# Output projections from seven block products, with their weight blocks split by three engines

## The reference, cut to what matters

```python
merged = sigmoid(a_r) * y_r + sigmoid(a_f) * y_f      # tokens x 1024, y = heads @ w_o
x = x + merged @ w_out[l]                             # 1024 x 1024 times 1024 x 1024
h2 = rmsnorm(x, g_ffn[l])                             # block 1: feeds the FFN
# block 2 ends with: return rmsnorm_2(x + merged @ w_out_2, final_norm_g_2)
```

## Time and profile before

| | us |
|---|---|
| median of 3 runs | 3062.49 |
| the profiled execution, its own time | 3061.24 |
| its span, first to last instruction | 3059.5 |
| TensorE busy | 2936.4 (96%) |
| VectorE, ScalarE, GpSimd busy | 1511.6, 1038.7, 946.5 |
| mean granted TensorE clock | 0.985 |

### The profile page before, as it was taken

How to read it: one execution, slowest core, us unless ns; L and a number is a source line. 1 busy time by engine, 2 the same in 40 slices (tenths; PEclk the granted TensorE clock), 3 DMA queues, 4 the chain that set the end, 5 groups by cost and what they waited for, 6 DMA issues and landing times.

```text
span 3059.5 us, 38358 instructions
## 1 busy us (share of the span) xinstructions
PE 2936.4 (96%) x14282; PEld 2348.0 (77%) x14282; DVE 1511.6 (49%) x2003; ACT 1038.7 (34%) x1732; POOL 946.5 (31%) x725
## 2 busy tenths in 40 slices
PE   7989999999999999999998999999999999999998
PEld 6778777788787788887887766668788888788886
...
GB/s 128 42 43 59 18 28 18 93 45 48 60 95 136 92 83 81 78 90 195 48 46 129 97 8 21 15 40 104 83 76 80 82 71 80 73 158 48 45 110 86
DMA packets 107877, 224.13 MB, mean 73 GB/s; under 512 B 14048, under 2 KB 27104, under 8 KB 106848
## 3 DMA queue, kind: packets, MB, share of 16 engines
q1 hardware_dynamic: 67680, 134.01, 14.5%
...
...
## 4 chain that ended last, share of the span: by engine, by line
PE 78%; DVE 12%; ACT 5%; issue 2%; POOL 2%; DMA 1%; ACTq 0%; POOLq 0%; SPq 0%; DVEq 0%
PE ps L356 17%; PE ps L372 13%; PE ps L2050 12%; PE ps L317 12%; PE ps L2172 8%; PE ps L1085 3%; PE ps L1116 1%; PE ps L2376 1%; DVE mla_ptl L1049 1%; ACT ps L1025 1%; PE ps L1101 1%; DVE mla_nm L1058 1%; PE ps L1103 1%; PE ps L1102 1%; POOL wl L3379 1%
## 5 line engine op out<-in xcount | busy, mean ns | idle before, releaser
L3377 POOL TENSOR_TENSOR wh<-raw,zeros 128x512 fp32r<-128x512 f32 x356 | 400.5, 1125 | 2077.7 <-PE ps L372 559.2
L3379 POOL TENSOR_TENSOR wl<-raw,wh 128x512 fp32r<-128x512 f32 x356 | 532.8, 1497 | 27.9
L372 PE MATMUL ps<-hth,wh 128*128 128x512 f32 x704 | 285.3, 405 | 2.1 <-DVE fox_vl L1298 2.1
L372 PE MATMUL ps<-hth,wl 128*128 128x512 f32 x704 | 279.2, 397 | 0.0
L372 PE MATMUL ps<-htl,wh 128*128 128x512 f32 x704 | 278.8, 396 | 0.0
L317 PE MATMUL ps<-wh,hth 128*128 128x512 f32 (+2 forms) x608 | 237.3, 390 | 12.4 <-POOL wl L3379 7.7
L317 PE MATMUL ps<-wl,hth 128*128 128x512 f32 (+2 forms) x608 | 234.1, 385 | 0.0
L317 PE MATMUL ps<-wh,htl 128*128 128x512 f32 (+2 forms) x608 | 233.8, 385 | 0.0
L356 PE MATMUL ps<-hth,wh 128*128 128x512 f32 x496 | 196.6, 396 | 0.4 <-issue 0.3
L356 PE MATMUL ps<-hth,wl 128*128 128x512 f32 x496 | 196.3, 396 | 0.0
L356 PE MATMUL ps<-htl,wh 128*128 128x512 f32 x496 | 196.2, 395 | 0.0
...
## 6 DMA issues: line engine op xcount, KB each, us to landing
raw<-in_stream_dram SPq DMA_DIRECT2D x356, 256.0 KB, 2.6
up_raw<-in_stream_dram SPq DMA_DIRECT2D x21, 1024.0 KB, 5.8
...
norm_x<-in_x_dram ACTq DMA_DIRECT2D x1, 4096.0 KB, 15.8
...
```

The source lines that it names most:

```text
L372: ins = nc.tensor.matmul(ps[:, bank + half, :], w[:, j, c:c + P], a[:, k, HALF * half:HALF * half + HALF], start=k == 0 and q == 0, stop=k ...
L3377: nc.gpsimd.tensor_tensor(wh[:, s, :], raw[:, s, :], zeros[:].to_broadcast([P, HALF]), ALU.add).then_inc(w_hi, 1)
L3379: nc.gpsimd.tensor_tensor(wl[:, s, :], raw[:, s, :], wh[:, s, :], ALU.subtract).then_inc(w_split, 1)
```

## The change

The projection is written as seven block products instead of eight. The merged activations have four blocks: P (features 0 to 511, tokens 0 to 511), Q (features 512 to 1023, the same tokens), R and S (the same for tokens 512 to 1023). The weight has e, f (rows 0 to 511, column half 0 and 1) and g, h (rows 512 to 1023). VectorE forms, in M and in new tiles, s1 = R+S, s2 = s1-Q, s3 = Q-S, s4 = P-s2, and w1 = h-g, w2 = f-w1, w3 = f-h, w4 = e-w2. The seven products are P e, Q g, s1 w1, s2 w2, s4 f, s3 w3, R w4, each of 4 feature groups x 4 token tiles x 3 = 48 matmuls, 336 in all; sums are formed in PSUM and in X.

Only e and f come through the stream and GpSimd (8 units for a projection, `U_OUT` 16 -> 8). The other five weight blocks (g, w1, w2, w3, w4) are split by ScalarE (`Wh`) and VectorE (`Wl`). TensorE's order of units of 12 matmuls is `SEQUENCE`; e alternates with g, and f with w2 and w3. f is loaded once beside the stream, for w2 and w3. h and g are loaded at the start of the merge stage (`early_loads`, g into slot 1 of `sg`) and subtracted there (`early_sum`, w1); ScalarE's second pair of sigmoids waits for that. g is loaded once more for its own split, h once more for w3, e for w4. The residual comes in two DMAs of 2 MB. The norm goes by halves of the tokens: tiles 4 to 7 take their second-half columns first. `Down` keeps its own order of transposes. Below, the diff cut to its core; `tt` is a tensor_tensor on VectorE (subtract unless it says add), `low(w, x, j)` waits for ScalarE's `h{w}.j` and makes `l{w}.j`, and removed bodies are those named above.

```diff
+def out_units(a):
+    for ks, c in ((K1, 0), (K1, 1)):
+        for k in ks:
+            unit(rows(a, k, HALF * c, HALF))
+out_units(w["w_out"][0])
...
+OUT_BLOCKS = N_UNITS + 4 * (PAIRED + 1)
+N_ALL = OUT_BLOCKS + 2 * 16
+K1, K2 = range(0, 4), range(4, 8)
...
+    self.Wh = sb(name + "_wh", [P, 4, HALF], F32R, scope)
+    self.Wl = sb(name + "_wl", [P, 4, HALF], F32R, scope)
+    self.Ml = sb(name + "_ml", [P, KT, S], F32R, scope)
+    self.S1h = sb(name + "_s1h", [P, 4, HALF], F32R, scope)
+    self.S2h = sb(name + "_s2h", [P, 4, HALF], F32R, scope)
...
+def late_square(self, act, summed, t, last):
+    summed(act, t, last)
+    n = len(self.squares)
+    if n >= 2:
+        self.a.wait(act, self.squares[-2])
+    self.squares.append(f"sq{last}.{t}")
+    self.a.did(nc.scalar.activation(self.junk[:, n % 2, :], self.X[:, t, self.later(t) if last else self.early(t)], ACT.Square,
+                                    accum_out=self.ss[:, last, t:t + 1]), f"sq{last}.{t}")
+def late_root(self, act, summed, t):
+    self.late_square(act, summed, t, 1)
+    self.a.wait(act, f"sq1.{t}")
+    self.v.wait(act, f"base{t // 4}")
+    self.a.did(nc.scalar.activation(self.r[:, 0, t:t + 1], self.ss[:, 1, t:t + 1], ACT.Sqrt, scale=1.0 / D, bias=self.base[:, t:t + 1]), f"rt{t}")
+def late_warm(self, act):
+    self.a.wait(act, "sq0.3")
+    self.a.did(nc.scalar.activation(self.r[:, 0, 0:1], self.ss[:, 0, 0:1], ACT.Sqrt), "warm")
+def late_base(self, dve, n):
+    ts = slice(4 * n, 4 * n + 4)
+    self.a.wait(dve, f"sq0.{4 * n + 3}")
+    self.v.did(nc.vector.tensor_scalar(self.base[:, ts], self.ss[:, 0, ts], 1.0 / D, EPS, ALU.mult, ALU.add), f"base{n}")
+def late_gains(self, dve, ts):
+    if ts[0] == 0:
+        dve.wait_ge(self.gain_in, 16)
+    for t in ts:
+        at = self.X[:, t, self.early(t)]
+        self.v.did(nc.vector.tensor_tensor(at, at, self.G[:, self.early(t)], ALU.mult), f"xg{t}")
...
-    self.pa.wait(act, "a1", KT - 1)
-    for k in range(KT):
-        self.v.wait(act, "sum", k)
-        nc.scalar.activation(hth[:, k, :], self.M[:, k, :], ACT.Copy).then_inc(self.ch, 1)
...
+SEQUENCE = ("e0 g0 e1 g1 e2 g2 e3 g3 w1.0 w1.1 w1.2 w1.3 w2.0 w2.1 f0 w2.2 f1 w2.3 f2 w3.0 f3 w3.1 w3.2 w3.3").split()
+PRODUCT = dict(e="pe", g="qg", w1="s1w1", w2="s2w2", f="s4f", w3="s3w3")
...
+    self.P, self.Q, self.R, self.S = M[:, 0:4, t1], M[:, 4:8, t1], M[:, 0:4, t2], M[:, 4:8, t2]
+    self.f = norm.XN[:].rearrange("p a (b n) -> p (a b) n", b=2)
+    self.low = lambda k: norm.Ml[:, 4 * (k // 2):4 * (k // 2) + 4, (t1, t2)[k % 2]]
...
+def early_loads(self, act):
+    act.dma_start(self.norm.F[:], self.weights(K2, 1)).then_inc(self.early_in, 16)
+    for br in range(2):
+        act.dma_start(self.merge.sg[:, br, 1, :].rearrange("p (a n) -> p a n", a=2), self.weights(K2[2 * br:2 * br + 2], 0)).then_inc(self.early_in, 16)
+def early_sum(self, dve):
+    dve.wait_ge(self.early_in, 48)
+    for br in range(2):
+        at = self.norm.F[:, 2 * br:2 * br + 2, :]
+        self.v.did(nc.vector.tensor_tensor(at, at, self.merge.sg[:, br, 1, :].rearrange("p (a n) -> p a n", a=2), ALU.subtract), "w1" + "ab"[br])
+def g(self, br):
+    return self.merge.sg[:, br, 0, :].rearrange("p (a n) -> p a n", a=2)
+def early_summed(self, act):
+    self.v.wait(act, "w1b")
+    a, v, p, m, n = self.a, self.v, self.p, self.merge, self.norm
+    def copy(out, x, step):
+        a.did(nc.scalar.activation(out, x, ACT.Copy), step)
+    def high(w, x, j, product):
+        if product:
+            p.wait(act, f"{product}.u{j}" if j < 3 else f"{product}.3")
+        copy(n.Wh[:, j, :], x[:, j, :], f"h{w}.{j}")
+    last = KT - 1
+    m.pa.wait(act, "a1", last)
+    for k in range(last):
+        m.v.wait(act, "sum", k)
+        to = slice(0, S if k < 4 else HALF)
+        copy(hth[:, k, to], m.M[:, k, to], f"hi{k}")
+    for br in range(2):
+        act.dma_start(self.g(br), self.weights(K2[2 * br:2 * br + 2], 0)).then_inc(self.g_in, 16)
+    m.py.wait(act, "y0", last)
+    act.dma_start(n.X[:, 0:4, :], self.source[:, 0:4, :]).then_inc(self.x_in[0], 16)
+    act.wait_ge(self.g_in, 32)
+    m.py.wait(act, "y1", last)
+    act.dma_start(self.f, self.weights(K1, 1)).then_inc(self.f_in, 16)
+    for j in range(4):
+        copy(n.Wh[:, j, :], self.g(j // 2)[:, j % 2, :], f"hg.{j}")
+    m.v.wait(act, "sum", last)
+    copy(hth[:, last, 0:HALF], m.M[:, last, 0:HALF], f"hi{last}")
+    v.wait(act, "s1b")
+    copy(n.S1h[:], self.R, "s1h")
+    high("w1", n.F, 0, "qg")
+    v.wait(act, "s3b")
+    copy(hth[:, 4:8, HALF:S], self.S, "s3h")
+    n.load(act)
+    act.dma_start(n.X[:, 4:8, :], self.source[:, 4:8, :]).then_inc(self.x_in[1], 16)
+    high("w1", n.F, 1, "qg")
+    v.wait(act, "lg.3")
+    copy(n.S2h[:], self.Q, "s2h")
+    high("w1", n.F, 2, "qg")
+    high("w1", n.F, 3, "qg")
+    v.wait(act, "w2")
+    high("w2", n.F, 0, "s1w1")
+    for t in range(4):
+        n.late_square(act, self.summed, t, 0)
+    high("w2", n.F, 1, "s1w1")
+    high("w2", n.F, 2, "s1w1")
+    p.wait(act, "s1w1.3")
+    act.dma_start(self.R, self.weights(K2, 1)).then_inc(self.h_in, 16)
+    copy(n.S1h[:], self.P, "s4h")
+    v.wait(act, "s3l")
+    act.dma_start(self.S, self.weights(K1, 0)).then_inc(self.e_in, 16)
+    high("w2", n.F, 3, "s1w1")
+    n.late_warm(act)
+    v.wait(act, "w3")
+    for j in range(4):
+        high("w3", self.R, j, "s2w2")
+    for t in range(4):
+        n.late_root(act, self.summed, t)
+    for j, t in ((0, None), (1, 0), (2, None), (3, 1), (None, 2), (None, 3)):
+        if j is not None:
+            high("w4", self.S, j, "s3w3")
+        if t is not None and not n.final:
+            n.high(act, t)
+            self.store(act, t)
+    for t in range(4, NT):
+        n.late_square(act, self.summed, t, 0)
+    if n.final:
+        for t in range(4, NT):
+            n.late_root(act, self.summed, t)
+        return
+    for t in range(4, NT):
+        n.late_root(act, self.summed, t)
+        if t > 4:
+            n.high(act, t - 1)
+            self.store(act, t - 1)
+    n.high(act, last)
+    self.store(act, last)
...
+    def add(k, t):
+        bank, tile, c = dict(pe=(0, 0, 0), qg=(4, 0, 0), s1w1=(0, 4, 1), s2w2=(4, 0, 1), s4f=(0, 0, 1), s3w3=(4, 4, 1), rw4=(4, 4, 0))[k]
+        p.wait(dve, f"{k}.{t}")
+        at = n.X[:, tile + t, HALF * c:HALF * c + HALF]
+        tt(at, at, ps[:, bank + t, :], f"{k}.{t}", ALU.add)
+    for k in range(4):
+        a.wait(dve, f"hi{k}")
+        tt(htl[:, k, :], M[:, k, :], hth[:, k, :], f"lo{k}")
+    m.column(dve, KT - 2, 0, M[:, KT - 2, :])
+    m.v.wait(dve, "sum", KT - 2)
+    v.wait(dve, "lo3")
+    tt(M[:, 0:3, t2], M[:, 0:3, t2], M[:, 4:7, t2], "s1a", ALU.add)
+    v.wait(dve, "s1a")
+    tt(M[:, 4:7, t2], M[:, 4:7, t1], M[:, 4:7, t2], "s3a")
+    m.gated(dve, last, 1, M[:, last, :], 0)
+    a.wait(dve, "hi6")
+    tt(htl[:, 4:7, t1], M[:, 4:7, t1], hth[:, 4:7, t1], "loqa")
+    m.gated(dve, last, 1, M[:, last, :], 1)
+    low_g(0)
+    m.total(dve, last, M[:, last, :])
+    low_g(1)
+    m.v.wait(dve, "sum", last)
+    tt(M[:, 3, t2], M[:, 3, t2], M[:, 7, t2], "s1b", ALU.add)
+    a.wait(dve, "hi7")
+    tt(htl[:, 7, t1], M[:, 7, t1], hth[:, 7, t1], "loqb")
+    v.wait(dve, "s1b")
+    tt(M[:, 7, t2], M[:, 7, t1], M[:, 7, t2], "s3b")
+    v.wait(dve, "s3b")
+    tt(self.Q, self.R, self.Q, "s2")
+    low_g(2)
+    a.wait(dve, "s1h")
+    v.wait(dve, "s2")
+    tt(self.low(1), self.R, n.S1h[:], "s1l")
+    low_g(3)
+    low("w1", n.F, 0)
+    low("w1", n.F, 1)
+    tt(self.P, self.P, self.Q, "s4")
+    a.wait(dve, "s2h")
+    v.wait(dve, "s4")
+    tt(self.low(2), self.Q, n.S2h[:], "s2l")
+    low("w1", n.F, 2)
+    dve.wait_ge(self.x_in[0], 16)
+    for t in range(4):
+        add("pe", t)
+    low("w1", n.F, 3)
+    dve.wait_ge(self.f_in, 16)
+    v.wait(dve, "lw1.3")
+    tt(n.F[:], self.f, n.F[:], "w2")
+    for t in range(4):
+        v.wait(dve, f"pe.{t}")
+        add("qg", t)
+    v.wait(dve, "w2")
+    for j in range(3):
+        low("w2", n.F, j)
+    a.wait(dve, "s3h")
+    tt(htl[:, 4:8, t2], self.S, hth[:, 4:8, t2], "s3l")
+    dve.wait_ge(self.x_in[1], 16)
+    for t in range(4):
+        add("s1w1", t)
+    a.wait(dve, "s4h")
+    tt(self.low(0), self.P, n.S1h[:], "s4l")
+    low("w2", n.F, 3)
+    dve.wait_ge(self.e_in, 16)
+    tt(self.S, self.S, n.F[:], "w4")
+    dve.wait_ge(self.h_in, 16)
+    tt(self.R, self.f, self.R, "w3")
+    n.late_base(dve, 0)
+    if n.final:
+        n.late_gains(dve, range(4))
+    v.wait(dve, "w3")
+    for j in range(3):
+        low("w3", self.R, j)
+    for t in range(4):
+        add("s2w2", t)
+    low("w3", self.R, 3)
...
+    if n.final:
+        for t in range(4):
+            whole("s4f", t)
+            if t:
+                n.scaled(dve, t - 1)
+        for j in range(3):
+            low("w4", self.S, j)
+        n.scaled(dve, 3)
+        for t in range(4):
+            add("s3w3", t)
+        low("w4", self.S, 3)
+        n.late_base(dve, 1)
```

(113 more changed lines are left out.)

199 lines of the change are left out of this document (98 added, 101 removed).

## The result

| | before | after |
|---|---|---|
| median of 5 runs, us | 3062.25 (3060.23 to 3066.68) | 3046.78 (3043.97 to 3049.07) |
| profiled execution, own time / span | 3061.24 / 3059.5 | 3046.78 / 3044.7 |
| mean granted clock | 0.985 | 0.988 |

What follows compares the result with a forecast made beforehand. TensorE's matmuls were taken to bound the changed stretches, the tail of out2 being set by GpSimd. Out1 -7.0, out2 -1.8 and merge2 +1.0 sum to -7.8 from 3061.24, forecast 3053 us, range 3037 to 3067.

Steps and rivals of the forecast that it cites:

- forecast case: Whole kernel: the summed terms hold, about 3053 us, in the band 3046 to 3057; chance 0.45.
- Step 1: Both projections: one block product taken out, 48 matmuls at 0.2333 us, 11.2 us less in each.
- Step 2: End of out1: old waits and slow clock go (-5.5), a new wait for tile 4's scaling comes (+3.5); net -2.0 us.
- Step 3: End of out2: the last four tiles' serial chain makes a tail of 11.8 us against 11.7; -0.5 us taken.
- Step 4: Both projections: VectorE's queue, slowed by GpSimd's turns, makes TensorE wait before w1.0 and run at lower clock; +5.8 us each.
- the slower rival: VectorE and GpSimd are overrun: TensorE's waits outgrow the gain, e units late at e2 and e3; 3076 us, chance 0.13.
- Step 5: Later in VectorE's queue: e's load, w4, w3 and gains delay the s2w2 adds; +0.4 us in out1, +4.1 in out2.
- Step 6: Start of merge2: column 1's sigmoids wait for the early loads and subtractions; +1.0 us, bounds 0 and 5.
- VectorE keeping up: Rival: GpSimd's turns cost VectorE less than its 4 us cover, no wait at w1.0 or w3.0; 3037 us, chance 0.22.
- The overrun: Rival: waits of 17.7 us per projection and 4 in merge2 exceed the gain; 3076 us, half as deep 3066; chance 0.13.

Runs made afterwards that it cites:

- x5: Against the changed kernel, end of out1: squares of tiles 4 to 7, base1 and tile 4's scaling moved ahead of copies and low parts of earlier tiles; 3045.15 us.
- x1: Against the changed kernel, VectorE makes s2's low part and lw1.2 behind the four P e adds in both projections; 3040.43 us, ratio 0.9926.
- x2: Against the changed kernel, GpSimd leaves out the low parts of the projections' sixteen units; 3034.73 us, ratio 0.9915.
- x6: Against the changed kernel, the VectorE orders of x1 and x3 together, and s4's low part ahead of s3's; 3042.35 us, ratio 0.9937.
- x3: Against the changed kernel, VectorE makes w3 ahead of w4, with w4 and out2's four gains behind the s2w2 adds; 3045.31 us, ratio 0.9945.
- x7: Changed kernel plus x5, x6, tail adds ahead of the last tile's scaling, last half tile on ScalarE, merge2's early loads issued sooner; 3032.97 us, ratio 0.9900.

## Why the prediction was right or wrong

The kind was right: the matmuls bring what they cost, and about half of it is paid back at waits on VectorE, at the places named. The sum was 6.7 us too small, in sizes, and 3046.78 stands at the very edge of the forecast case (3046 to 3057).

**Step 1**, 48 matmuls for 11.2 us in each projection: right. out2 spent 86.38 us on 335 distances; less its waits (2.73 + 2.07 + 0.25) and 2.9 of slow matmuls, 78.4 us are left, 0.234 each.

**Step 2**, end of out1, -2.0: it was -3.7. The 5.5 us went. The wait before tile 4 came at the place named and for the reason named (x5), but at 1.82 instead of 3.5. Its chain from the transpose of tile 3 took 920.07 - 912.34 = 7.7 us and not 8.4, and 5.9 us of matmuls lay beside it and not 4.9, because I left out the transpose itself.

**Step 3**, tail of out2, -0.5: it was -1.9. The prediction's own sum was a tail of 11.8; it measured 9.8. Each tile took 2.66 us (2.8 forecast), 0.6 less for four. The chain's first add (3029.41) stood 5.5 us ahead of TensorE's last matmul, forecast 4.2: 1.3 less. The last half on GpSimd began with VectorE's last scaling (0.06 us behind it) and not after its end, 0.7 less, and took 2.12 instead of 1.6, 0.5 more. The store took 3.1 as said.

**Step 4**, the term that decides, 5.8 in each: 4.2 in out1 (0.59 + 2.18 + 1.4) and 4.1 in out2 (2.73 + 1.4). The mechanism is shown by x1 (order) and x2 (whose time). The term mis-sized is VectorE's loss to GpSimd: the adds started at T + 24.6 and T + 24.3, where 26.1 was forecast. m1 ended at T + 1.5 in out1 (1.8 forecast). Of the 23.1 us from there to the add 6.7 were lost to GpSimd, 8.3 forecast, and 16.4 were VectorE's own work, 16.0 forecast. The prediction took the four low and three high parts at their full length; a low part cost 1.1 of its 1.30 us, a high part about 0.75 of its 1.04. GpSimd was slowed by more than the 1.5 to 2 times that were forecast: 2.85 us for 1.04 and 3.2 for 1.30. The sum of this step also has a slip: arriving at T + 23.4 for an add that ends at T + 26.7 is a wait of 3.3, not 3.5. And the 1.24 us in its reading of the earlier trace rows is counted from 2949.87, the start of the next VectorE instruction; the sum itself ended at 2949.94.

The rule that the Trainium skill states (SBUF — State Buffer, "Who interferes with whom"), an exclusive lock for whole instructions, is borne out by the trace: GpSimd's 1.30 us became 3.23 where it began 0.95 us into a 2048-column operation of 3.02, and it ended 1.16 us after that. The unit that it would make late, left to the slower rival at e2 and e3, did not come there; it came at f1 in x6, 6.2 us long, once the waits that hid it were gone.

**Step 5**: out1 0.4 forecast, none there; out2 4.1 forecast, 3.6 measured at w3.0 (2.07 + 1.5) and 0.25 at the last product. x3 shows its cause as it was put, the load of e, w4 and the gains ahead of the adds, taken together. The wait also went in x1 and x2, which leave that order alone, so it hangs on the whole backlog.

**Step 6**, +1.0: 0.93, right in size. x6 and x7 show that the loads set it.

**Not in the prediction**: about 1 us of the 11.6 in out1 that no wait and no fall of the clock accounts for, its cause open; 1.2 us less ahead of out1, inside the 828.4 to 832.9 us at which out1 begins in the nine profiles of changed kernels; and between the projections 2.9 us more, of which 0.93 is step 6, 1.5 are slow matmuls in the feed-forward part, behind a wait that both kernels have, and the rest variation.

Summed, against the forecast: out1 -4.6, out2 -3.1, ahead of out1 -1.2, between the projections +1.9, outside the span +0.3, together -6.7.

Of the rivals, VectorE keeping up (3037) was what x1 and x6 came near to by the order of the queue, and x2 by leaving out GpSimd's low parts; in the kernel as forecast there was no such slack. The overrun never showed. Its price "half as deep, +4 to +6" doesn't follow: half of 39.4 is 19.7, which is 5 less than the gain of 24.9.
